# H 32 bytes past a multiple of 64: two neighbours in SBUF change places

## The reference, cut to what matters

```python
for l in range(DEPTH):
    h = rmsnorm(x, norm1_g[l])
    x = x + gated_parallel_mixer(h, w_in[l], ...)     # z = h @ w_in, three attentions, three gates, w_out
    h = rmsnorm(x, norm2_g[l])
    x = x + conv_ffn(h, w_up[l], ..., w_down[l])      # (gelu(g) * a) @ w_down, a and g from h @ w_up
```

## The kernel before, in words

| tile | place | past a multiple of 64 | past a multiple of 128 |
|---|---|---|---|
| wraw, whi, wlo (all) | from 16512 on | 0 | 0 |
| X | 98432 | 0 | 0 |
| H | 106624 | 0 | 0 |
| c1 | 123008 | 0 | 0 |
| par | 124576 | 32 | 32 |
| y0 | 138880 | 0 | 0 |
| cqn, ckn (high and low) | 169824 to 178016 | 32 | 96 |
| y1, y2 | 184160, 192352 | 32 | 96 |
| fh, fl, gh, gl | 134272, 156800, 142464, 175232 | 0 | 0 |

## Time and profile before

### The profile page before, as it was taken

One profiled execution on the slowest core, in us unless ns is written; L12 is line 12 of the kernel. 1 busy time (PEld: TensorE's weight loads), 2 busy tenths in 40 slices (PEclk: granted clock), 3 DMA queues, 4 the chain that ended last, 5 costly groups with the idle time before them and its releaser, 6 DMA issues.

```text
span 1703.3 us, 29657 instructions
## 1 busy us (share of the span) xinstructions
PE 1626.7 (96%) x12312; PEld 1472.0 (86%) x12312; DVE 1131.2 (66%) x1806; ACT 906.6 (53%) x1431; POOL 302.9 (18%) x222
## 2 busy tenths in 40 slices
PE   6999999999999999999999997899999899899998
PEld 5899998999898999999988986778888789878886
DVE  4575656877457655568755586479845776789844
ACT  4656855665447576566644644345633444456531
POOL 0000120343000002104410242016400200007400
PEclk9999999999999999999999998999999999999999
DMA  5634354555564434636554622025654434235652
GB/s 198 198 114 149 125 186 157 206 184 184 189 179 145 146 116 150 218 129 219 175 186 161 249 88 76 28 78 199 237 195 160 173 124 149 99 145 199 229 193 75
DMA packets 45253, 272.97 MB, mean 160 GB/s; under 512 B 4672, under 2 KB 8896, under 8 KB 16064
## 3 DMA queue, kind: packets, MB, share of 16 engines
q1 hardware_dynamic: 44400, 266.36, 45.6%
q10 hardware_dynamic: 720, 4.72, 0.8%
HBM read 270.01 MB, written 1.05 MB: 159 GB/s over the span
## 4 chain that ended last, share of the span: by engine, by line
PE 77%; DVE 11%; ACT 6%; DMA 3%; issue 2%; SPq 0%; POOL 0%; DVEq 0%; ACTq 0%; POOLq 0%
PE b_ps L358 11%; PE b_ps L360 11%; PE b_ps L361 11%; PE b_ps L434 9%; PE b_ps L437 8%; PE b_ps L435 8%; PE b_ps L404 6%; DVE b_wlo L315 4%; PE b_ps L405 3%; DMA b_wraw<-in_w 3%; ACT b_S L911 2%; ACT b_whi L307 1%; PE b_ps L1001 1%; PE b_ps L1911 1%; PE b_ps L938 1%
## 5 line engine op out<-in xcount | busy, mean ns | idle before, releaser
L315 DVE TENSOR_TENSOR b_wlo<-b_wraw,b_whi 128x2048 fp32r<-128x2048 f32 (+1 forms) x264 | 574.0, 2178 | 198.5 <-PE b_ps L437 128.2
L307 ACT ACTIVATE b_whi<-b_wraw 128x2048 fp32r<-128x2048 f32 (+1 forms) x264 | 469.3, 1779 | 216.9 <-PE b_ps L437 152.1
L358 PE MATMUL b_ps<-b_H,b_whi 128*128 128x256 f32 x1784 | 516.4, 289 | 9.9 <-ACT b_zrot L785 6.3
L360 PE MATMUL b_ps<-b_H,b_whi 128*128 128x256 f32 x1784 | 506.5, 284 | 0.0
L361 PE MATMUL b_ps<-b_H,b_wlo 128*128 128x256 f32 x1784 | 506.5, 284 | 0.0
L358 PEld LDWEIGHTS b_ps<-b_H,b_whi 128*128 128x128 f32 x1784 | 343.6, 193 | 18.5 <-ACT b_zrot L785 6.7
L360 PEld LDWEIGHTS b_ps<-b_H,b_whi 128*128 128x128 f32 x1784 | 343.8, 193 | 0.9
L361 PEld LDWEIGHTS b_ps<-b_H,b_wlo 128*128 128x128 f32 x1784 | 343.8, 193 | 0.0
L404 PE MATMUL b_ps<-b_H,b_whi 128*128 128x512 f32 x448 | 155.8, 393 | 0.0
L1480 POOL TENSOR_TENSOR b_fl<-b_ab,b_fh 128x256 fp32r<-128x256 f32 x44 | 93.8, 2131 | 219.3 <-ACT b_fh L1453 219.3
L405 PE MATMUL b_ps<-b_H,b_wlo 128*128 128x256 f32 x448 | 124.8, 279 | 0.0
(11 more groups left out here) (352 smaller groups left out, 2781.2 us busy)
## 6 DMA issues: line engine op xcount, KB each, us to landing
b_wraw<-in_w SPq DMA_DIRECT2D x223, 1024.0 KB, 4.9
b_wraw<-in_w SPq DMA_DIRECT2D x37, 512.0 KB, 3.6
b_bias<-in_rpb SPq DMA_DIRECT2D x8, 512.0 KB, 10.0
b_gains<-in_gains ACTq DMA_DIRECT2D x4, 1024.0 KB, 4.9
b_wraw<-in_w SPq DMA_DIRECT2D x2, 768.0 KB, 4.3
b_cA<-in_cA SPq DMA_DIRECT2D x2, 576.0 KB, 7.6
b_X<-in_x SPq DMA_DIRECT2D x2, 512.0 KB, 4.9
out<-b_X SPq DMA_DIRECT2D x4, 256.0 KB, 2.6
```

The costliest lines, as they stand in the source:

```text
L307: e.activation(whi[u % NHI][:, 0:n], raw[u % NRAW][:, 0:n], ACT.Copy).then_inc(up("w_hi", "whi", u))
L315: e.tensor_tensor(wlo[u % NLO][:, 0:n], raw[u % NRAW][:, 0:n], hi.bitcast(F32), ALU.subtract).then_inc(up("w_lo", "wlo", u))
L358: e.matmul(out, wh, x.hi[:, kk, :], start=k == 0, stop=False)
L360: e.matmul(out, wh, x.lo[:, kk, :], start=False, stop=False)
```

## The change

c1 is allocated ahead of H instead of behind it.

```diff
     X = sb(top, "X", [P, 2, D])
+    c1 = sb(top, "c1", [P, sum(w for _, w in at1.values())])
     H2 = sb(top, "H", [P, 8, 2, T], F32R)
     Hh, Hl = H2[:, :, 0, :], H2[:, :, 1, :]
-    c1 = sb(top, "c1", [P, sum(w for _, w in at1.values())])
     par = sb(top, "par", [P, atP[1]])
```

## The result

The changed kernel takes 1694.04 us (median of six runs, 1693.23 to 1699.2 us) against 1705.68 us for the kernel before (median of six, 1703.97 to 1708.35 us). The ratio is 0.9939, with a 95% interval from 0.9924 to 0.9954: 10.4 us faster, and 7.8 to 13.0 us by the interval (the two medians themselves lie 11.6 us apart). Forecast were 5.7 us, and 1702 us with a range down to 1698 us. The sign was right and the size was not; the time lies outside the range. Part of the distance to it is the base: the forecast counted from 1707.38 us, 1.7 us above the median of six. The range's lower end is a gain of 9.4 us, which the interval of the gain takes in; the forecast gain of 5.7 us is outside of it.

What follows compares the result with a forecast made beforehand. The prediction took TensorE to bound the kernel. Its terms, -7.5 + 3.2 - 1.4 = -5.7 us, with nothing for ScalarE and VectorE, took 1707.38 us to 1701.7, stated as 1702 us, range 1698 to 1709.

Steps and rivals of the forecast that it cites:

- What bounds the kernel: Whole kernel: TensorE, busy 1626.7 of 1703.3 us, sets the time; its mixer idle time should grow by about 1 us.
- Part 1: H as moving operand, 256 columns, 5352 matmuls: 1.6 ns saved on each, 7.5 us saved on the path.
- The term of 8.6 us: H's 5352 moving matmuls at 1.6 ns each: 8.6 us of TensorE time saved, before the path's share.
- share of 0.87: Part of H's moving matmul time taken to be on the path: 562 of 642 us.
- Part 2: H as stationary operand, 512 moving columns, 160 triples: 22 ns more each, 3.2 us lost.
- the forecast's last part: Signs expected in the changed timeline; triples with H as weights should take 700 ns in place of 680.
- Part 3: 448 MLP pairs, with 512 and 256 columns of H: 1.6 ns saved per matmul, 1.4 us saved.
- first rival: MLP pairs pay like the 512-column value rows, +2.9 us; sum -1.4 us, 1706 us; chance 0.20.
- Part 4: Writers and readers of H on ScalarE and VectorE, 64 each: at most 0.6 us, taken as nothing.
- third rival: How moving stream and weight load lie to each other counts; slower, about 1743 us or, milder, 1713.5 us; chance 0.12.
- second rival: Nothing happens, since a shift by 32 bytes crosses no more 16-byte lines: 1707.4 us; chance 0.08.

Runs made afterwards that it cites:

- h_minus32: Kernel before with H moved by 224 bytes, to 32 below the weights' place, other distances kept modulo 256; ratio 0.9987 to the kernel before.
- all_inputs_plus32: Changed kernel with y0, y1, y2, cqn and ckn also 32 above the weights' place modulo 256; ratio 0.9946 to the kernel before.
- all_plus32: Kernel before with 32 unused bytes ahead of every tile, so all places move and all distances stay; ratio 0.9997.
- p256_h32: Kernel before with H moved by 32 bytes inside a tile 256 bytes larger, other distances kept modulo 256; ratio 0.9952.
- h_off64: Kernel before with H moved by 64 bytes and everything behind H by 128 bytes; ratio 1.0024.
- h_off16: Kernel before with H moved by 16 bytes and everything behind H by 128 bytes; ratio 0.9996.
- p256_h16: Kernel before with H moved by 16 bytes inside a tile 256 bytes larger, other distances kept modulo 256; ratio 0.9947.
- w_off32: Kernel before with H kept in place and both rings of weights, whi and wlo, moved by 32 bytes; ratio 1.0074.

## Why the prediction was wrong in size and right in sign

**What bounds the kernel**: right. TensorE's starts set the time of the FFN and MLP stretches before and after, and 11.6 of the 12.7 us that TensorE saved came out of the span. Idle time in the mixers, of which 1 us more was forecast, is 19.8 us instead of 19.7 in the first one; a growth of that size is below what executions differ by.

**Part 1** is the step that failed: "Those of the third branch read y2, 32 past one: 24 starts in 2.84 us, 118.3 ns. That is a difference of 1.7 ns by the offset alone". y2 lies 32 past a multiple of 64, and so does the moved H; but y2 is 32 *below* the weights modulo 256, and H came to lie 32 *above* them. h_minus32 puts H where y2 is and gets the 118.3 ns of the forecast; all_inputs_plus32 puts y2 where H is and gets 116.7 ns. The offset modulo 64 was the wrong measure: all_plus32 has it and gains nothing. The term of 8.6 us of TensorE time measures 15.5 us. The same part has a slip that the size of the price hides: its share of 0.87 sets the chain's 562 us in the lines L358, L360 and L361 against H's 5352 matmuls alone, but these lines have 6084 matmuls, y and the latents included, so that the same working gives 562 / 730 = 0.77. What the share was can't be read from one pair of executions: 11.6 of 12.7 us of busy time (0.91) for the change, 9.5 of 13.5 us (0.70) for p256_h32, which has the same paces.

**Part 2**: right in kind and nearly in size. A triple takes 700 ns, as the forecast's last part said, and the bill over the whole trace is 2.6 us of the 3.2 us forecast. (The three lines hold 25% of the chain by the earlier trace rows, not 26%; nothing was worked out from it.) This too is a matter of distance: the output products pay, 17.5 or 22.5 ns a triple, when it is they that lie 128 or 96 off.

**Part 3**: the sign was right, but not the reason. -0.4 ns a pair instead of -3.2. That 512 columns behave like 256 because the surcharge is the same at distance 0 was a poor argument: at -32 the pair pays 5.8 ns. The first rival's price for it (6.4 ns) would have been near at that distance.

**Part 4**: nothing visible. The subtraction into H takes 418 ns on the mean instead of 421, the copy on ScalarE 419 instead of 420; VectorE's busy time differs by 0.6 us and ScalarE's by 2.7 us over the whole kernel, on engines with a third and more of their time idle.

**Rivals.** The third rival named the mechanism, "how the moving stream and the weight load lie to each other", and that the reference tiles all lie 96 past a multiple of 128. It was right that this hid an unknown, but I gave the unknown one sign only. The first rival's sum (-1.4 us, with the pairs paying) is close to what H at -32 does: 2.2 us (0.3 to 4.1). The second rival rested on the Trainium skill (SBUF — State Buffer, the cachelines under "Door 1"): by that rule alone no run should differ in which tiles move by whole multiples of 16 bytes. They differ, from 113.3 to 120.0 ns, so here the measurement decides against it as the only cost. The same page (under "Who interferes with whom") calls TensorE's read ports for the moving operand and for the weights independent and says that it never waits on anyone. No run here shows the ports, and waiting for another engine is not what was measured; but the two reads are not independent in their effect, since the moving stream's starts go from 120.0 to 116.7 ns with the distance of its two operands.

**What stays open.** That a pace goes by the distance of the two streams is shown. Why is not: that the reads of a weight load and those of the moving stream meet in the same part of the memory is an idea that fits, and no run looks inside. Whether the distance to whi or to wlo counts could not be told apart, since both rings lie at the same place modulo 256. Why h_off64 and h_off16 take longer than their paces add up to, and what picks the pace at +16, is open as well. A layout that keeps the gain of H moving and avoids the 2.6 us of H stationary wasn't tried; it needs the weights of those products 32 bytes further on in the rings than the others.

## What to carry to other kernels

When TensorE bounds a kernel, its pace in steady state can depend by some per cent on where the operands lie to each other (2.8% here between distance 0 and +32, with 256 moving columns); read it as the distance of starts over 24 matmuls in a stretch without gaps, not as a mean duration. A tile moved by a few bytes changes the distances of all tiles behind it as well, so an experiment on places needs a control, and here 256 unused bytes are neutral while 128 are not (7.5 us of TensorE time in the output products). And a row that is to price another tile must agree with it in everything that may count, here in the sign and period of its distance, not only in the property that the change is named after.

## What the runs showed of the hardware that I had not expected

- The same 256-column float32r matmul starts every 113.3, 116.7, 118.3 or 120.0 ns, at the upper clock, by the distance of its two operands in SBUF modulo 256. With 512 columns of weights moving and the other tile stationary it is the other way round: distance 0 is the best seen (226.7 ns), and 96 costs 7.5 ns (w_off32, 12 starts in 2.81 us). The MLP's pairs follow a third pattern: on the mean they take 347 ns at 0, +16 and +32, 350 ns at +48 and +96, and 353 ns at +8, +64 and -32.
- At a distance of 16 bytes the two FFNs of one execution ran at different steady paces, 118.8 and 116.7 ns (p256_h16), and one FFN changed from 116.7 to 113.3 ns behind a few small matmuls (h_off16). So the place does not fix the pace alone. That it is how a stretch is entered which counts is a guess that fits this and the kernel before, where H needed eight starts (0.94 us, about 118 ns) before it settled at 120.0 ns; no run tests it.
